# Summing 28 late modulation vectors between the attention's steps instead of beside the q, k, v products

## The reference

```python
def ada_mod(cond, w, b):
    m = (jax.nn.silu(cond) @ w + b)[..., None, :]
    return jnp.split(m, 6, axis=-1)
...
sh1, sc1, g1, sh2, sc2, g2 = ada_mod(c, ada_w[i], ada_b[i])
csh1, csc1, cg1, csh2, csc2, cg2 = ada_mod(c_ctx, ada_w[i], ada_b[i])
...
lat = lat + g1 * y_lat
lat = lat + g2 * conv_ffn(modulate(rms_norm(lat, norm2_g[i]), sh2, sc2),
                          ffn_w_up[i], ffn_conv_w[i], ffn_w_down[i])
```

## Time and profile before

| | |
|---|---|
| time, median of 3 runs | 3448.14 us |
| the profiled execution's own time | 3456.3 us |
| its span, first to last instruction | 3454.5 us |
| busy: PE, DVE, ACT, POOL | 79%, 45%, 29%, 25% of the span |
| mean granted TensorE clock | 0.885 of full speed |

### The profile page before, as it was taken

How to read it: one execution, slowest core, us unless ns; L and a number is a source line. 1 busy time by engine, 2 the same in 40 slices (tenths; PEclk the granted TensorE clock), 3 DMA queues, 4 the chain that set the end, 5 groups by cost and what they waited for, 6 DMA issues and landing times. The chain is left out here.

```text
span 3454.5 us, 60891 instructions
## 1 busy us (share of the span) xinstructions
PE 2720.1 (79%) x24644; PEld 2217.0 (64%) x24644; DVE 1543.4 (45%) x2385; ACT 1016.5 (29%) x1530; POOL 851.4 (25%) x490
## 2 busy tenths in 40 slices
PE   2568657958758375688587877999999799889998
PEld 2555435837648265577476866888888664467886
DVE  7766723853363326456435434431441334335142
ACT  2231312242222213121521234431221442245232
POOL 3311103204013213022021132232233220144444
PEclk9887768959779687789798989999999899999999
DMA  4420005400000113244000031121121210122222
GB/s 164 163 68 1 1 38 178 169 9 3 3 2 4 62 49 143 98 173 146 9 3 2 3 122 49 61 67 59 63 70 34 87 46 1 60 68 96 93 92 91
DMA packets 61191, 228.64 MB, mean 66 GB/s; under 512 B 5568, under 2 KB 11840, under 8 KB 58816
## 3 DMA queue, kind: packets, MB, share of 16 engines
q1 hardware_dynamic: 60992, 225.76, 18.9%
HBM read 212.10 MB, written 13.63 MB: 65 GB/s over the span
## 5 line engine op out<-in xcount | busy, mean ns | idle before, releaser
L2559 POOL TENSOR_TENSOR f_wl<-f_stage,f_wh 128x1024 fp32r<-128x1024 f32 (+1 forms) x120 | 316.1, 2634 | 616.5 <-ACT f_wh L2555 616.5
L2555 ACT ACTIVATE f_wh<-f_stage 128x1024 fp32r<-128x1024 f32 (+1 forms) x120 | 137.6, 1146 | 594.2 <-PE f_ps L2642 593.0
L2642 PE MATMUL f_ps<-h_h,f_wh 128*128 128x256 f32 (+1 forms) x704 | 238.3, 340 | 17.4 <-POOL f_wl L2559 13.2
L2642 PE MATMUL f_ps<-h_l,f_wh 128*128 128x256 f32 (+1 forms) x704 | 237.5, 339 | 0.0
L2642 PE MATMUL f_ps<-h_h,f_wl 128*128 128x256 f32 (+1 forms) x704 | 237.4, 339 | 0.0
L2847 DVE SCALAR_TENSOR_TENSOR f_xr<-f_ps,cols,f_xr 128x511 f32<-128x511 f32 (+1 forms) x132 | 83.1, 657 | 339.5 <-ACT f_xr L2840 339.0
L2642 PE MATMUL f_ps<-f_f_ah,f_wh 128*128 128x512 f32 (+1 forms) x528 | 183.6, 355 | 0.0
L2642 PE MATMUL f_ps<-f_f_ah,f_wl 128*128 128x512 f32 (+1 forms) x528 | 183.5, 354 | 0.0
L2642 PE MATMUL f_ps<-f_f_al,f_wh 128*128 128x512 f32 (+1 forms) x528 | 183.4, 354 | 0.0
L2642 PEld LDWEIGHTS f_ps<-h_h,f_wh 128*128 128x128 f32 x704 | 132.8, 189 | 36.0 <-POOL f_wl L2559 14.3
L2642 PE MATMUL f_ps<-hc_h,f_wh 128*128 128x512 f32 x352 | 142.6, 405 | 13.4 <-POOL f_wl L2559 12.9
(11 more groups left out here) (661 smaller groups left out, 7177.1 us busy)
## 6 DMA issues: line engine op xcount, KB each, us to landing
f_stage<-in_ffn_up SPq DMA_DIRECT2D x88, 512.0 KB, 3.5
f_stage<-in_ffn_down SPq DMA_DIRECT2D x32, 704.0 KB, 4.0
p_hgrn_mm_side_w<-in_ada_w SPq DMA_DIRECT2D x12, 1024.0 KB, 5.1
qkv_mm_side_w<-in_ada_w SPq DMA_DIRECT2D x12, 1024.0 KB, 5.0
u_mm_side_w<-in_ada_w SPq DMA_DIRECT2D x11, 1024.0 KB, 4.9
mod_w<-in_mod_w SPq DMA_DIRECT2D x8, 1024.0 KB, 14.3
a_uv_mm_side_w<-in_ada_w SPq DMA_DIRECT2D x8, 1024.0 KB, 5.4
p_hgrn_mm_stage<-in_w_in SPq DMA_DIRECT2D x12, 512.0 KB, 4.9
```

The costliest lines, as they stand in the source:

```text
L2555: self.nc.scalar.activation(self.wh[:, slot, :w], self.stage[:, slot, :w], ACT.Copy).then_inc(self.w_high, 1)
L2559: self.nc.gpsimd.tensor_tensor(self.wl[:, slot, :w], self.stage[:, slot, :w], self.wh[:, slot, :w].bitcast(F32), ALU.subtract).then_inc(se ...
L2642: done = self.nc.tensor.matmul(out[s][:, :tn], w, x[:, k, t0:t0 + tn], start=k == 0 and n == 0, stop=k == job.kt - 1 and n == 2)
```

## The change

Three of the five `Gemv` uses of the second block change: `a_uv_mm` now makes vectors 48 to 63 (two a tile), `b_gate_mm` 64 to 67 (one a tile), and `qkv_mm` none. The other 28, 68 to 95, are made in the attention: SP loads the condition vectors and then one vector's rows per step, ACT applies Silu ahead of the first exponential, and DVE does the two sums at the end of each of the first 28 steps. It waits for the Silu once, ahead of the first reciprocal.

The modulation is split to match: 20 vectors and one scale where it was, 28 and the other scale in a new stage between attention and `c_out`. In all `Gemv` uses the second sum's product is written over the rows that it reads, which halves `side_junk`.

```diff
@@ class Gemv
-        self.junk = st.sbuf("side_junk", [P, 2, D])
+        self.junk = st.sbuf("side_junk", [P, D])
...
+    def credits(self, dve):
+        dve.sem_inc(self.used, 2)
+        dve.sem_inc(self.summed, 2)
...
-                nc.vector.scalar_tensor_tensor(self.junk[:, j, :], self.rows[:, slot, g, :], 1.0, self.conds[:, j, :],
+                junk = self.rows[:, slot, g, :] if j else self.junk[:, :]
+                nc.vector.scalar_tensor_tensor(junk, self.rows[:, slot, g, :], 1.0, self.conds[:, j, :],
                                                ALU.mult, ALU.mult, accum_out=out).then_inc(self.summed, 1)
@@ def attention
+        side.place(st)
         block = st.block()
+
+        @block.sync
+        def _(sp):
+            side.load_vec(sp)
+            for n in range(n_side):
+                side.load(sp, n, n % 2)
...
+            side.silu(nc, act)
             exponential(0)
...
+            side.credits(dve)
             maximum(0)
+            dve.wait_ge(side.vec_ok, 1)
             for n, (h, q) in enumerate(jobs):
...
                 if q == 0 and h:
                     low_part(h - 1)
+                if n < n_side:
+                    side.sums(nc, dve, n, n % 2)
             low_part(HEADS - 1)
@@ def second
-                  warm=ACT.Gelu, also=[(x_dram, x2[:, :, :])], side=Gemv(d["ada_w"], d["vec_2"], mods, 72, 2))
+                  warm=ACT.Gelu, also=[(x_dram, x2[:, :, :])], side=Gemv(d["ada_w"], d["vec_2"], mods, 48, 2))
...
-                  side=Gemv(d["ada_w"], d["vec_2"], mods, 88, 2))
+                  side=Gemv(d["ada_w"], d["vec_2"], mods, 64, 1))
...
-                  side=Gemv(d["ada_w"], d["vec_2"], mods, 48, 2), also=[(gate_dram, gate[:, :, :])])
+                  also=[(gate_dram, gate[:, :, :])])
...
-            modulation(nc, t, "mods2", 48, cols_of(t, "ada_b_2")[:, 48:], (56, 80), (gains1[:, KD:], gains2[:, KD:]))
+            modulation(nc, t, "mods2", 48, cols_of(t, "ada_b_2")[:, 48:68], (56,), (gains1[:, KD:],))
...
-            attention(nc, t, qn, qr, kn, kr[:, 0, :], v, hh[:, :, :LAT], hl[:, :, :LAT])
+            attention(nc, t, qn, qr, kn, kr[:, 0, :], v, hh[:, :, :LAT], hl[:, :, :LAT],
+                      Gemv(d["ada_w"], d["vec_2"], mods, 68, 1), 28)
+        modulation(nc, t, "mods2", 68, cols_of(t, "ada_b_2")[:, 68:], (80,), (gains2[:, KD:],))
```

More of the change, by code:

```diff
@@ L3311, in _, with attention @@
                 nc.vector.tensor_tensor(x, x, part[:, :], ALU.add).then_inc(rope_ok, 1)
-def attention(nc, t, qn, qr, kn, kr, vtok, oh, ol):
+def attention(nc, t, qn, qr, kn, kr, vtok, oh, ol, side, n_side):
     QT = LAT // P
```

## The result

The changed kernel takes 3507.7 us, the median of four runs, against 3448.1 for the kernel before beside it: a ratio of 1.017, with an interval of [1.0109, 1.0232]. The prediction was 3473.8 with a range of 3464 to 3484. The sign is right, the size is not: +59.6 us against +25.7. The four runs also lie far apart, where those of the kernel before lie within 4.4 us, and the mean granted TensorE clock goes with them: 3488.4 us at 0.881, 3495.5 at 0.879, 3519.8 and 3522.9 at 0.871. The profiled execution is the one of 3522.9.

What follows compares the result with a forecast made beforehand. The prediction took PE to bound the attention and the q, k, v products. Its terms, 24.2 + 3.0 + 1.4 - 0.5 - 2.4 = +25.7 us on 3448.1, gave 3473.8 us, range 3464 to 3484.

Steps and rivals of the forecast that it cites:

- The step that failed: Attention: PE's 3.98 us of work per step stays as it is, under a DVE chain of 4.91 us.
- Rival 2: Attention: PE idles about 1 us per step, so TensorE's clock falls to 1.2 GHz; +144, 3593 us; chance 0.04.
- The chain on DVE: Attention: sums lengthen DVE's chain per step, +0.93 us ordinary, +1.70 behind a head's product; +24.2 us in sum.
- The start: Attention's start: condition vectors' transfer, Silu and table loads delay the first exponential; +3.0 us, bounds 1.8 to 4.4.
- The modulations: New stage between attention and c_out costs +1.4 us; the old modulation loses two operations, -0.5 us.
- The q, k, v products: Their start: first product comes sooner without 1024 KB of vectors ahead of the first weights; -2.4 us.
- The rows' transfers: Attention: each load is wanted 7.2 us after issue, 1024 KB land in 4.8 us, so no cost.
- Rival 1: Attention: sums ride in DVE's idle time, so the kernel isn't slower; +1.5, 3449.6 us; chance 0.06.
- Rival 3: Attention: the sum writing over its own rows is slow, twice 1.15 us; adds 24 us, 3498 us; chance 0.05.

Runs made afterwards that it cites:

- e2_dve_only: Kernel before plus only two sums at the end of each of the attention's first 28 steps, on data already in SBUF, results unused; 3476.3 us, ratio 1.0071.
- e5_spare_start: Changed kernel plus unneeded PE products before transposes of steps not first of their head, and six ahead of the first transposes; 3468.8 us, ratio 1.0055.
- e9_rows_unread: Kernel before plus the start's transfer, Silu and wait, serial in-place sums on other operands, and 28 row transfers nobody reads; 3496.0 us, ratio 1.0119.
- e1_spare: Changed kernel plus unneeded PE products before transposes of each step not first of its head, none at the attention's start; 3481.6 us, ratio 1.0087.
- e3_start_only: Kernel before plus only the attention's new start (condition vectors' transfer, Silu, wait), no sums; 3468.0 us, ratio 1.0059.
- e4_one_sum: Changed kernel with each attention step's second sum over 8 elements instead of 1024; 3462.4 us, ratio 1.0035.
- e7: Changed kernel run again without alteration, for a second profile; 3486.5 and 3528.6 us, ratio 1.0161.
- e6: Kernel before plus the attention's new start and two sums a step for 28 steps on data already there, no row transfers; 3480.6 us, ratio 1.0091.
- e10: Kernel before plus the new start and sums whose second waits for the first and writes over the same buffer, no row transfers; 3497.5 us, ratio 1.0156.
- e11_serial_pair: Kernel before plus sums whose second waits for the first and writes over the same buffer, without new start or row transfers; 3482.8 us, ratio 1.0091.

## Why the prediction was wrong

- **The step that failed** is that TensorE keeps 2.4 GHz in the attention, so that its work of 3.98 us hides under a chain of 4.9. In the changed kernel's profile the clock was 0.72, and 48 of the attention's 70 us come from that (229.0 against 180.7 with PE kept busy). By the earlier trace rows a busy share of 0.82 had gone with a clock of 1.00. That window had its gaps spread among 546 short products; here PE stands in one piece for 1.55 us, and the window from another stage didn't stand for it. That the gaps' form is the reason is argued and not shown: e2_dve_only kept 1.00 in its profile with waits of 1.44 us in one piece.
- **Rival 2** was the right mechanism with the wrong form: I priced it as all or nothing, 3593 us, gave it 0.04, and allowed a dip of 1 to 3 us behind the start. It came as a swing: low from about 1 us behind the start of the transposes that had waited 1.55 us until some 2 us ahead of the next head's product, 17 of a head's 30.7 us. The price of 3593 was also 24 us too low by its own terms: counted from the kernel before, which has no such waits to take off, the stage's 168 us once more are +168 and not +144, and give 3618. The rule cited there from the Trainium skill (TensorE: Matmul & The Clock Gate, "A second HAM failure mode: psum-queue depth-cycling"), a PE that idles briefly between groups and swings between both clocks, describes what the trace shows, clock 0.50 and 1.00 in turns and 0.72 over the attention.
- **The chain on DVE**, +24.2, was right in mechanism and a little large. With the clock held, the steps are 4.77 us (forecast 4.91), 5.53 behind a product (5.62) and 9.23 into one (9.22): +21.9 in e5_spare_start. The pair takes 2.51 us instead of 2.60.
- **The start**, +3.0, measured +4.4 to +4.5, just at the bound of 4.4: the vectors land 5.9 us after their issue, not 4.8, and are issued 1.07 us behind ACT's last work and not 0.77. The two table loads cost 1.28 us each with no gap, as the rows said.
- **The modulations** +1.4 and -0.5: measured +1.5 and -0.5. **The q, k, v products** -2.4: measured -2.2, and 1.1 in b_gate_mm besides. **The rows' transfers**: nobody waited for them.
- **Rival 1** fell: a chain of 4.77 us is over 3.98. **Rival 3** fell: the sum over its own rows takes 1.22 us like the other.
- With the clock held, the same change measures 3468.8, +19.0 beside its own kernel before. The forecast was 5 us above that, so the whole of the error of 34 us is the clock. The terms as measured (21.9 + 4.4 + 1.5 - 0.5 - 2.2 - 1.1 = 24.0) would have given 5 us more than these 19.0; that lies within what the stages ahead of the attention vary by chance, and stays open.

What stays open: why the same waits seem to bring falls in one execution and not in another; why the changed kernel's profiles have deeper falls (229) than e9_rows_unread (198.8), which has its sums, start and transfers with other operands (in the changed kernel each of heads 1 to 6 takes the same steps and has its one long low stretch at the same place, in e9_rows_unread most low stretches are a step long and their places differ from head to head); and what part of the medians of e1_spare and e3_start_only their profiles don't show.

## What to carry to other kernels

Where a change makes TensorE wait in one piece at regular places (here for 1.55 us once a head), price the clock as a term of its own, up to the engine's own work in the stretch once more, and not as a remote rival; and where the runs then spread, compare their mean clocks. A few useless products in place of the wait can hold the clock: here they made the changed kernel 39 us faster. Idle DVE time under a busy PE is no room if DVE's work stands in a chain that PE waits for. What the first product of a stage needs should be issued first: that alone was worth 0.5%.

## What was not expected of the hardware

- PE at 1.2 GHz, recorded as busy for 100% of the time, stayed there for 26 us in the changed kernel (2821 to 2847), in steps of 7.48 us. It was not the head's product that brought it back: the clock rose some 1.8 us ahead of it, and in e4_one_sum nearly 6 us ahead. In e3_start_only the same steps, after the same kind of start, were back at 2.4 GHz in 4 us. What sorts the profiles is small: the wait ahead of the first transposes was 4.31 to 4.36 us in the three profiles that stayed low (changed, e4, e7) and 3.85 to 4.16 in the five that came back within a step (e1, e3, e6, e9, e10). Whether this is the reason isn't shown.
- The waits behind a head's product of the profiles with falls in nearly every head (1.55 us) and of those with few or none (1.44 us) lie 0.11 us apart. Between e2_dve_only and e11_serial_pair the attention grew by 17.7 us (178.6 to 196.3, one profile each), of which the pairs themselves make some 2.
- Transfers at 75 GB/s beside the products changed neither the clock nor a duration (0.87 and 198.7 us against 0.87 and 198.8).
